# Recurrence of block 1: one unread product with 256 columns ahead of each level's first products

## The reference, cut to what matters

```python
def step(s, inp):
    rt, wt, kt, vt, at, bt = inp
    sa = jnp.einsum('bhvk,bhk->bhv', s, at)
    s = s * wt[:, :, None, :] + sa[..., None] * bt[:, :, None, :] + vt[..., None] * kt[:, :, None, :]
    y = jnp.einsum('bhvk,bhk->bhv', s, rt) if return_y else None
    return s, y
```

## Time and profile before

| | |
|---|---|
| runs | 3533.66, 3539.24 and 3531.85 us; median 3533.66 us |
| the profiled execution | 3547.03 us, with a span of 3545.2 us from the first to the last instruction |
| granted clock of TensorE over the span | 0.952 of full speed |
| busy in the span | PE 91%, PEld 72%, DVE 54%, ACT 35%, POOL 5% |
| the recurrence of block 1 | from 390 to 805 us of the span |

### The profile page before, as it was taken

One profiled execution on the slowest core, in us unless ns is written; L12 is line 12 of the kernel. 1 busy time (PEld: TensorE's weight loads), 2 busy tenths in 40 slices (PEclk: granted clock), 3 DMA queues, 4 the chain that ended last, 5 costly groups with the idle time before them and its releaser, 6 DMA issues.

```text
span 3545.2 us, 61398 instructions
## 1 busy us (share of the span) xinstructions
PE 3214.5 (91%) x26760; PEld 2565.7 (72%) x26760; DVE 1925.4 (54%) x2832; ACT 1255.5 (35%) x2068; POOL 171.8 (5%) x167
## 2 busy tenths in 40 slices
PE   6998788889798887699999799999999999899999
PEld 4866677775443333699888568998899887579997
DVE  3356665555321112788342748873887344658863
ACT  3226433331100000454232655443543333654432
POOL 0003221230100000000000000000000000000000
PEclk8989888899899999899999999999999999899999
DMA  6240000014599997232241012323232331013322
GB/s 229 72 143 22 2 3 3 3 35 179 222 383 421 421 421 322 85 108 93 104 148 66 13 60 72 108 96 131 72 108 96 131 113 60 1 60 94 104 94 83
DMA packets 174022, 441.53 MB, mean 125 GB/s; under 512 B 5954, under 2 KB 97852, under 8 KB 149180
## 3 DMA queue, kind: packets, MB, share of 16 engines
q1 hardware_dynamic: 173756, 437.61, 33.4%
HBM read 435.49 MB, written 2.10 MB: 123 GB/s over the span
## 4 chain that ended last, share of the span: by engine, by line
PE 68%; DVE 9%; DMA 7%; ACT 3%; issue 3%; SPq 0%; DVEq 0%; ACTq 0%
PE banks L338 8%; PE banks L3137 7%; PE banks L3140 7%; PE banks L3139 7%; PE banks L2309 6%; PE banks L3258 4%; PE banks L3259 4%; PE banks L3257 4%; DMA ring<-in_exp_w_gate 3%; DMA ring<-in_exp_w_up 2%; PE banks L1512 1%; PE banks L380 1%; DMA ring<-in_exp_w_down 1%; PE banks L334 1%; PE banks L1535 1%
## 5 line engine op out<-in xcount | busy, mean ns | idle before, releaser
L2309 PE MATMUL banks<-ring,arena 128*64 128x512 f32 x1120 | 265.7, 617 | 43.3 <-DMA ring<-in_exp_w_gate 19.5
L3259 PE MATMUL banks<-tail_r,hid_r 128*128 128x512 f32 x704 | 279.7, 397 | 0.0
L3258 PE MATMUL banks<-ring_r,two_r 128*128 128x512 f32 x640 | 254.0, 397 | 0.0
L3257 PE MATMUL banks<-tail_r,two_r 128*128 128x512 f32 x640 | 250.7, 392 | 0.0
L2309 PEld LDWEIGHTS banks<-ring,arena 128*64 128x64 f32 x1120 | 91.5, 142 | 204.3 <-issue 186.0
L3137 PE MATMUL banks<-ring_r,tail_r 128*128 128x256 f32 x624 | 175.6, 281 | 9.0 <-DVE arena L3222 9.0
L295 DVE TENSOR_TENSOR hid_r<-arena,two_r 128x1024 fp32r<-128x1024 f32 x40 | 49.0, 1226 | 238.1 <-ACT two_r L292 223.8
L3139 PE MATMUL banks<-ring_r,tail_r 128*128 128x256 f32 x624 | 175.9, 282 | 0.0
L3137 PE MATMUL banks<-mix_r,tail_r 128*128 128x256 f32 x624 | 175.5, 281 | 0.0
L3139 PE MATMUL banks<-h_r,tail_r 128*128 128x256 f32 x624 | 174.7, 280 | 0.0
L3140 PE MATMUL banks<-mix_r,ring_r 128*128 128x256 f32 x608 | 171.2, 282 | 0.0
(11 more groups left out here) (546 smaller groups left out, 8842.3 us busy)
## 6 DMA issues: line engine op xcount, KB each, us to landing
ring<-in_exp_w_gate SPq DMA_DIRECT2D x31, 2048.0 KB, 17.2
ring<-in_w_ffn_gate SPq DMA_DIRECT2D x44, 1024.0 KB, 5.4
ring<-in_w_ffn_up SPq DMA_DIRECT2D x44, 1024.0 KB, 5.4
ring<-in_exp_w_down SPq DMA_DIRECT2D x20, 2048.0 KB, 17.6
ring<-in_w_ffn_down SPq DMA_DIRECT2D x20, 2048.0 KB, 7.9
ring<-in_exp_w_up SPq DMA_DIRECT2D x19, 2048.0 KB, 16.2
ring<-in_w_in SPq DMA_DIRECT2D x17, 2048.0 KB, 10.2
arena<-in_exp_w_up SPq DMA_DIRECT2D x13, 2048.0 KB, 18.7
```

Of the source, the lines that this page charges most:

```text
L2309: ins = TE.matmul(banks[64 * e:64 * e + 64, b0 + hf, :], lhs(kk, e), w[:, k, hf * 512:(hf + 1) * 512], start=(kk == 0), stop=(kk == KD - 1))
L3257: TE.matmul(bank, h_hi, w_hi[:, c, ns], start=(f == 0), stop=False)
L3258: TE.matmul(bank, h_hi, w_lo[:, c, ns], start=False, stop=False)
L3259: ins = TE.matmul(bank, h_lo, w_hi[:, c, ns], start=False, stop=(f == NF - 1))
```

## The change

A helper `unread(d)` is added to `step_pe`. It multiplies the identity with the 256 mask columns of direction `d` and writes the result to the upper half of bank 4 + d, where nothing reads it. It is called at the start of `level_p` for levels 2, 3 and 4 and at the start of `pair_p`, each time ahead of the waits: 8 calls in each step, 48 in the kernel. It signals nothing.

```diff
+                        def unread(d):
+
+                            TE.matmul(lower(d)[:, 256:512], ident, masks[:, d, :], start=True, stop=True)
+
                         def level_p(i, d):
 
+                            if i > 1:
+                                unread(d)
                             l.wait_ge(*past(co, "Al", i, d))
                             l.wait_ge(*past(co, "XT", i - 1, d))
                             if n and i == 1:
...
                         def pair_p(d):
 
+                            unread(d)
                             l.wait_ge(*past(co, "XT", 4, d))
                             l.wait_ge(*past(co, "Amf", d, 1))
                             for g in range(8 * d, 8 * d + 8):
```

## The result

The changed kernel is slower: 3546.36 us against 3539.86 us for the kernel before, medians of 19 runs each, a ratio of 1.0022 with a 95% interval from 1.0012 to 1.0032. With 19 runs the kernel before shows a higher median than with the three that stood ahead of the prediction; the ratio is what counts. A second measurement, among the experiments, gave 1.0025 (1.0010 to 1.0041).

The account below looks back on a forecast made before the run. Instruction fetching was taken to bound the levels, the slow clock the tails. Uncovered calls 6.3 plus instructions 2.1 less returned clock 9 gave -0.6 us: 3546.4 profiled, 3533.0 as median, range 3520 to 3546.

Parts of the forecast that it names:

- The price of one call: TensorE's time for each added product at the full clock: 0.35 us, 16.8 us for 48 calls (13 to 24).
- The upper end, 0.50: Highest price of a call, from a full 128-column product at 0.124 us, doubled for twice the columns: 0.25 a record.
- What the stops cover: Calls before instruction-fetch stops in levels 2 to 4 cost nothing, five of eight per step; the uncovered three cost 6.3 us.
- The instructions' 2.1 us: Fetching the added instructions in the levels, 24 a step at 3.8 us per 256: 2.1 us, between 0 and 2.9.
- a shift of the packets: In later parts, 192 added instructions move packets by three quarters of one; costed at nothing.
- The clock: Fewer clock falls in level and tail stretches: 9 us returned, two thirds of 13.4; from nothing to the whole.
- the slower rival: Clock not moved, calls on the path: 8.4 us with five of eight covered, 18.9 with none; chance 0.22.
- point of decision: The slower rival decides when under 8.4 of the 13.4 us of clock loss comes back.
- tail stretches: Pairs and halves, behind the levels: those of steps 1 and 4 were to take near 11 us.
- level stretches: Levels 1 to 4 of each step: were to take near 27 to 28 us for all steps.
- 27.0 taken as a floor: Shortest time for levels 1 to 4 at full clock, set by fetching; stretches under 27 us would show it wrong.
- The packet's pace: While products are small, TensorE can't go faster than one fetched packet of 256 instructions in 3.8 us.

Follow-up runs that it names:

- twice: The changed kernel with each of the 48 calls made twice; 3564.91 us against 3544.46 for the kernel before.
- level_one_only: The changed kernel with its calls replaced by four per step ahead of level 1's wait for GpSimd; 3545.46 us against 3543.98 for the kernel before.
- pairs_only: The changed kernel with only the 12 calls ahead of the pairs; 3549.36 us against 3544.46 for the kernel before.
- levels_only: The changed kernel with only the 36 calls of levels 2 to 4; 3538.35 us against 3544.46 for the kernel before.
- tiny: The changed kernel with 32 moving columns per call instead of 256, all 48 calls kept; 3549.62 us against 3544.46 for the kernel before.
- half_cols: The changed kernel with 128 moving columns per call instead of 256; 3548.35 us against 3543.98 for the kernel before.
- phase_128: The kernel before plus 32 small unread products in step 0, shifting later packets by half a packet; 3548.73 us against 3543.98 for the kernel before.
- levels_again: The 36 calls of levels 2 to 4 alone, measured a second time; 3540.13 us against 3542.74 for the kernel before.
- change_again: The changed kernel, unedited, measured once more; 3552.85 us against 3542.74 for the kernel before, ratio 1.0025.

## Why the prediction was wrong

**The price of one call is the term that failed.** The prediction put a call at 0.35 us, 16.8 us in all, between 13 and 24; measured are 0.52 to 0.62 at the full clock and 1.15 at the lower, some 30 us in all if the clock is full throughout. The misreading is in the gram products of the earlier trace rows. "8 records in 1.06 us, 0.132 each" is not the length of a 256-column record: their weights lie in alternating halves of 64 rows, and in the trace the records start in pairs, less than 0.01 us apart, with 0.21 us from pair to pair. A rate of 0.132 per record therefore stands for 2 x 0.132 = 0.26 us per pair and 0.53 for two, which is what a call costs. The value taken, 0.35, has half of that rate in it: 0.066 of the 0.176 per record. The upper end, 0.50, was above the streaming (0.43) and had left out what a change between full-width and small products costs: some 0.1 us behind a call, and another 0.1 ahead of it where small products stand there. So even the upper bound, 24 us, was too low.

**What the stops cover was right in us, not as a rule.** Forecast: 30 calls of 0.35 us, 10.5. The stops in front of the two level lines fell by 11.7 and 7.1 in the two profiles. The prediction had a call in front of a stop cost nothing; with calls nearly twice as long the stops gave no more than that, and `twice` gained hardly anything on top (13.5 us for 96 calls). So 30 less 12 or 7 leaves 18 or 23 where 8.4 had been forecast, and the runs show 18.4 and 20.6 at an equal clock. By parts: the pairs pay everything (0.68 per call), as forecast, the levels 0.29.

**The instructions' 2.1 us are too small to be seen.** At an equal clock the runs have 1.1 (1.5) with 32 columns and -0.8 (1.5) for a shift by half a packet. But both kernels had 20 us more of the low clock than before and took 5 us longer. The prediction put a shift of the packets at nothing, and what it does to the clock is open.

**The clock was right in kind.** 9 us were forecast; the runs have 43 and 33 us less at the lower clock in two measurements, which at 0.32 are 14 and 11. Against its own session's runs of before the second is 29 us less, worth 9. The work that a call adds is what brings it back, since calls of 32 columns at the same places don't: 352 us of low clock against 289. That speaks against the rule of the Trainium skill (TensorE: Matmul & The Clock Gate, HAM oscillation) as the whole story: in the profile with 32 columns TensorE's stops shrank as much as with 256 (from 36.5 to 23.7 and 24.8 us), and the clock didn't rise. It came from the calls in the levels; the pairs' calls brought 6 (6).

**The sum.** 18.4 - 14 = +4 and 20.6 - 11 = +10 us against the runs of before pooled over the sessions of the experiments (these sums hold by the way the price is worked out, and don't confirm it); the two ratios, each against its own session, say +8 and +9. The forecast had 8.4 - 9. Of the 13.4 us between the forecast 3533.0 and the measured 3546.36, 6.2 are the median of the kernel before, which three runs had put too low, and the rest is the change. The outcome is that of the slower rival, and its sign came about by the price, not by its mechanism, a clock that doesn't move; that +8 is near the rival's 8.4 is luck. Its point of decision, under 8.4 us returned, was passed with 11 to 14; with the true price it would have stood at 18.

**Of the signs named:** instructions and stops came as said, the tail stretches of steps 1 and 4 at 11.95 instead of near 11, the level stretches at 26.6 to 30.2 instead of 27 to 28. The shortest, 26.6, is under the 27.0 taken as a floor, which the prediction had named as a sign against it; `level_one_only` has one of 26.3. The packet's pace as a floor holds only roughly.

## What to carry to other kernels

A filler product is cheap only where the engine would have stood still for another reason; price it from the start of the call to the start of what follows, and double any rate read from products that run side by side in halves of the array. Here the same call is just about worth its price in the levels, where only 0.29 us of its 0.62 is paid, and is lost in front of the pairs, where nothing covers it. Where many runs are at hand, take the granted clock out of them before two kernels are compared: 0.32 us per us explained two thirds of the variance between runs of one kernel. A price got in this way still needs a second measurement, such as a stretch that has the full clock in both kernels.

## What had not been expected

In the last step the clock fell during TensorE's densest work. Timeline stretches of the changed kernel, the products of the state and the output in step 5:

```profile
783.90:795.50 11.60, 10.82 (x118) 10.65 (x118) 8.50 (x12) 3.63 (x7) 6.13 (x5) 1.00 0.01 1
795.50:812.00 16.50, 16.50 (x78) 16.31 (x78) 2.62 (x5) 0.63 (x1) 0.00 (x0) 0.50 0.00 1
```

TensorE was busy for 16.50 of 16.50 us at 0.50, behind 11.6 us at the full clock with 10.82 busy. These are products with 64 and 128 moving columns. The fall is in 7 of the 14 profiles of this study and costs some 7 us each time (130.0 instead of 122.6 us for that part of the six steps); it is in neither the profile of before nor in those of pairs_only, the first levels_only, tiny, half_cols, twice and phase_128, and it is in that of levels_again, the same code as levels_only. It goes with the session more than with the edit: all four profiles of the session of change_again have it, and none of the four of the session of pairs_only. That such falls make up a large part of the spread between runs is a guess. What decides it stays open.
